# Final RMSNorm of a two-layer decoder trunk: square root on ScalarE and reciprocal on VectorE in place of logarithm and exponential on ScalarE

## The chip, the core and the metric

One core of a Trainium2 chip runs the whole program. The metric is the device time of one execution in microseconds (us), lower is better. The engines named below are TensorE (PE, and PEld for its weight loads), VectorE (DVE), ScalarE (ACT), GpSimd (POOL) and SyncE (SP, which here issues the stores of the output).

## The reference, cut to what matters

Two layers of token mixing, a SwiGLU FFN and a gated per-layer embedding are computed on a residual stream `x` of 1024 tokens by 1024 channels; a final RMSNorm then makes the output. Only the end of it matters here:

```python
def rmsnorm(x, g):
    xf = x.astype(jnp.float32)
    y = xf * lax.rsqrt(jnp.mean(xf * xf, axis=-1, keepdims=True) + EPS)
    return (y * g.astype(jnp.float32)).astype(x.dtype)

def hybrid_layer(...):
    ...
    hp = rmsnorm(x, norm_ple)
    x = x + jax.nn.sigmoid(hp @ w_ple_gate) * (p_i @ w_ple_proj)
    return x

def reference(...):
    for i in range(DEPTH):
        x = hybrid_layer(x, p[i], ...)
    return rmsnorm(x, norm_final)
```

## The kernel before

The residual stream lies in SBUF with channels on the partitions: `x` is 128 partitions by 8 channel chunks `c` by 1024 tokens. Tokens are worked on in two halves `h` of 512 (`hs(h)`). Each engine has its instructions in a fixed order, written out by hand, and they wait for one another by semaphores.

The last stage of a layer is `ple_gate`. TensorE makes 16 pieces of the gate, j = 0 to 15, in the order of `GATE_ORDER`: chunks 0 to 4 in both halves, then chunks 5, 6, 7 of half 0 (j = 10, 11, 12), then chunks 5, 6, 7 of half 1 (j = 13, 14, 15). A piece is 24 matmuls (eight chunks in three passes, L2194 to L2196). Each piece then goes back and forth between two engines:

- `gate_in(j)`, VectorE, L1233: the PSUM bank of the piece times the row scale, into `psg`;
- `gate_sigmoid(j)`, ScalarE, L1501: the sigmoid in place;
- `gate_out(j)`, VectorE, L1240 and L1242: the sigmoid times the embedding, added to `x`;
- `gate_square(j)`, ScalarE, L1508: the square of the new `x`, into one of two buffers;
- `gate_square(j)`, VectorE, L640 (`add_square`): the square added to `square_sum` of its half.

A matmul with a constant matrix sums `square_sum` over the partitions into a PSUM bank `aux`, which gives the mean of squares of every token of that half on all partitions: L2334 for half 0, and L2589 with the last two squares at L2592 for half 1.

In the last layer the final norm is woven into this stage. On ScalarE `root_half(DEPTH, 0, h)` makes `rstd[:, h, :]`, a tile of 128 by 512 in fp32, from the bank by two instructions: a logarithm with eps as its bias (L1488) and an exponential scaled by -0.5 (L1490). The signal `rstd_made` tells VectorE. On VectorE `result_part(h, chunks)` multiplies `x` by the gain and by `rstd` (L1256), one instruction for each chunk; after each SP stores 256 KB of the output (L2095). The orders are:

- ScalarE: squares 11 and 12, sigmoid 13, root of half 0, square 13, sigmoids 14 and 15, squares 14 and 15, root of half 1;
- VectorE: squares 11 and 12, `gate_in` 13, `gate_out` 13, results of half 0 for chunks 0 to 4, `gate_in` 14, `gate_out` 14, square 13, `gate_in` 15, result of chunk 5, `gate_out` 15, results of chunks 6 and 7, then all eight results of half 1.

ScalarE loads a table (ACT_TABLE_LOAD) ahead of a function that the loaded table doesn't hold; the program has no line for that, and the profile shows the load under the line of the function that needs it. VectorE has one other reciprocal in the program, L898, on a tile of 128 by 4 in the mLSTM part of each layer, between small instructions on the same tile (L893, L895, L906).

Of the kernel before, what the change touches and what calls it, by code (L numbers as in the profile page):

```python
# [10 lines left out]
ACT = mybir.ActivationFunctionType  # L11
# [7 lines left out]
DEPTH = 2  # L19
# [240 lines left out]
def build(nc, w_d, x_d, p_d, pos_d, const_d, par_d, early_d, out_d):  # L260
# [6 lines left out]
    with ExitStack() as ctx:  # L267
        def sb(name, shape, dt=F32):
            return ctx.enter_context(nc.sbuf_tensor(name, shape, dt))[:]

        def sem(name):
            return ctx.enter_context(nc.semaphore(name))
# [15 lines left out]
        rstd = sb("rstd", [P, 2, HALF])  # L288
# [69 lines left out]
        eps_c, one_c = small[:, 0:1], small[:, 1:2]  # L358
# [22 lines left out]
        aux_done = Signal(sem("aux_done"), AUX_FILLS)  # L381
# [37 lines left out]
        rstd_made = Signal(sem("token_rstd"), 6)  # L419
# [47 lines left out]
        def aux_at(L, name):  # L467

            return aux_done.at(L, AUX[name][1] + 1)

        def aux_read(name):

            return aux_emptied[AUX[name][0]].sem

        def aux_read_at(L, name):

            return aux_emptied[AUX[name][0]].at(L, AUX[name][2] + 1)
# [12 lines left out]
        def abank(name):  # L490
            return aux[:, AUX[name][0], :]

        def hs(half):
            return slice(HALF * half, HALF * half + HALF)
# [104 lines left out]
        def _(v):  # L599
# [651 lines left out]

            def result_part(h, chunks):

                v.wait_ge(rstd_made.sem, rstd_made.at(DEPTH, h + 1))
                for c in chunks:
                    v.scalar_tensor_tensor(x[:, c, hs(h)], x[:, c, hs(h)], mix_gain[:, c:c + 1], rstd[:, h, :],  # L1256
                                           ALU.mult, ALU.mult).then_inc(result, 1)

            def ple_gates(L):
# [25 lines left out]
                else:  # L1285
# [3 lines left out]
                    gate_in(L, 13)  # L1289
                    gate_out(L, 13)  # L1290
                    result_part(0, range(0, 5))
                    gate_in(L, 14)
                    gate_out(L, 14)
                    gate_square(L, 13)
                    gate_in(L, 15)
                    result_part(0, range(5, 6))
                    gate_out(L, 15)
                    result_part(0, range(6, 8))
                    result_part(1, range(KC))

# [61 lines left out]
            for L in range(DEPTH):  # L1362
                steps[0] = 0
                for item in MACRO:
# [55 lines left out]
                    elif what == "early_low":  # L1420
                        h = args[0]
# [5 lines left out]
                    elif what == "out_units":  # L1427
                        for part in reloaded:
                            v.wait_ge(part, L * 16 + 16)
                        for j in range(16):  # L1430
                            add_fill(L, U_OUT + j // 2, j % 2, j // 2, j % 2)
                            if j >= 1:
                                add_square(L, 0, j - 1)
                                c, h = divmod(j - 1, 2)
# [30 lines left out]
        def _(a):  # L1465
# [18 lines left out]
            def root_half(L, i, h):  # L1484

                name = ("row", i, h)
                a.wait_ge(aux_done.sem, aux_at(L, name))
                a.activation(rstd[:, h, :], abank(name), ACT.Ln, bias=eps_c).then_inc(aux_read(name), 1)  # L1488
                a.wait_ge(aux_read(name), aux_read_at(L, name))
                a.activation(rstd[:, h, :], rstd[:, h, :], ACT.Exp, scale=-0.5).then_inc(rstd_made.sem, 1)  # L1490

            def next_high(h, chunks):

                for c in chunks:
                    high_part(c, h, mix_gain[:, c:c + 1])

            def gate_sigmoid(L, j):

                m, h = GATE_ORDER[j]
                a.wait_ge(emptied[bank(U_GATE + m, h)].sem, emptied_at(L, U_GATE + m, h))  # L1500
                a.activation(psg[:, j % 2, :], psg[:, j % 2, :], ACT.Sigmoid).then_inc(ple_sig.sem, 1)  # L1501

            def gate_square(L, j):

                m, h = GATE_ORDER[j]
                a.wait_ge(x_ple.sem, x_ple.at(L, j + 1))
                a.wait_ge(sq_added.sem, sq_added.at(L, 32 + j - 1))
                a.activation(sqr[:, j % 2, :], x[:, m, hs(h)], ACT.Square).then_inc(sq_made.sem, 1)  # L1508

            def ple_gates(L):  # L1510

                for j in range(12):
                    m, h = GATE_ORDER[j]
                    if h == 0 and m <= 5:
                        units_high(L, U_GATE + m + 2)
                    gate_sigmoid(L, j)
                    if j >= 1:
                        gate_square(L, j - 1)
                gate_sigmoid(L, 12)
                if L < DEPTH - 1:  # L1520
                    next_high(0, range(0, 5))
                    gate_square(L, 11)
                    gate_sigmoid(L, 13)
                    units_high(L, UNITS)
                    next_high(0, range(5, 7))
                    gate_square(L, 12)
                    next_high(0, range(7, 8))
                    gate_sigmoid(L, 14)
                    units_high(L, UNITS + 1)
                    gate_square(L, 13)  # L1530
                    gate_sigmoid(L, 15)
                    gate_square(L, 14)
                    gate_square(L, 15)
                    next_high(1, range(KC))
                else:
                    gate_square(L, 11)
                    gate_square(L, 12)
                    gate_sigmoid(L, 13)
                    root_half(DEPTH, 0, 0)
                    gate_square(L, 13)  # L1540
                    gate_sigmoid(L, 14)
                    gate_sigmoid(L, 15)
                    gate_square(L, 14)
                    gate_square(L, 15)
                    root_half(DEPTH, 0, 1)

            def high_part(c, h, scale, to=None):

                a.activation(hh[:, c, hs(h)] if to is None else to, x[:, c, hs(h)], ACT.Copy,
                             scale=scale).then_inc(h_hi.sem, 1)  # L1550
# [14 lines left out]
            def units_high(L, last):  # L1565

                while told[0] <= UNITS * L + last and told[0] < UNITS * DEPTH:
                    l, u = divmod(told[0], UNITS)
                    raw_slot, value = LANDED[("unit", l, u)]
                    slot, held = TOOK[("unit", l, u)]  # L1570
                    n = columns(u)
                    for key in {k for k in held if k is not None}:
                        a.wait_ge(*consumed(key))
                    a.wait_ge(raw_landed[raw_slot], value)
                    to, whole = whi[:, slot, 0:n], raws[raw_slot][:, 0:n]
                    if u == U_GATES:
                        to = whi[:, slot, :].rearrange("p (k c) -> p k c", c=P)[:, :, 0:64]
                        whole = whole.rearrange("p (k c) -> p k c", c=64)
                    a.activation(to, whole, ACT.Copy).then_inc(unit_hi.sem, 1)  # L1579
                    told[0] += 1  # L1580
# [242 lines left out]
            for L in range(DEPTH):  # L1823
# [6 lines left out]
                for item in MACRO:  # L1830
# [15 lines left out]
                    elif what == "unit":  # L1846
# [9 lines left out]
                        if u == U_MQ + 1:  # L1856
# [5 lines left out]
                                         bias=one_c[0:MH]).then_inc(row_act.sem, 1)  # L1862
# [69 lines left out]
                    elif what == "pool":  # L1932
                        for j in range(2):
                            for h in range(2):
                                name = ("pm", j, h)
# [3 lines left out]
                    elif what == "turn":  # L1939
                        p = args[0]  # L1940
                        for h in range(2):
                            name = ("vt", p, h)
# [15 lines left out]
                    elif what == "ret_y":  # L1958
# [4 lines left out]
                        for h in range(2):  # L1963
                            name = ("ry", p, h)
# [6 lines left out]
                    elif what == "spread":  # L1971
                        p = args[0]
                        for h in range(2):
                            name = ("rv", p, h)
# [3 lines left out]
                        for h in range(2):  # L1978
                            name = ("rv", p, h)
                            a.wait_ge(aux_read(name), aux_read_at(L, name))  # L1980
                            a.activation(KZ[:, hs(h)], KZ[:, hs(h)], ACT.Exp, scale=-0.5).then_inc(ret_rstd.sem, 1)
                    elif what == "early_high":

                        h = args[0]
# [18 lines left out]
                    elif what == "out_units":  # L2003
                        a.wait_ge(h_ready.sem, h_ready.at(L, 32))
                        for j in range(16):
                            c, h = divmod(j, 2)
# [93 lines left out]
        def _(g):  # L2100
# [15 lines left out]
            def split(L, u):  # L2116
# [8 lines left out]
                if (L, u) == (0, 0):  # L2125

                    for q in range(2):
                        ks = slice(4 * q, 4 * q + 4)
                        hi, _, whole = gate_parts(ks, (0, raw_slot))
                        g.tensor_tensor(hi, whole, zero1[:, 0:1].unsqueeze(2).to_broadcast([P, 4, 64]),  # L2130
                                        ALU.add).then_inc(first_w, 1)
                        g.wait_ge(first_w, 2 * q + 1)
                        ins = gate_low(ks, (0, raw_slot))
                        ins.then_inc(first_w if q == 0 else weights_ready.sem, 1)
                    return
# [589 lines left out]
```

## Time and profile before

| What | us |
|---|---|
| time, median of 3 runs | 2439.54 (2439.28 to 2439.76) |
| time of the profiled execution | 2439.59 |
| span of the profiled execution, first to last instruction | 2437.8 |
| TensorE busy in it | 2414.3 (99%) |
| VectorE busy | 1529.6 (63%) |
| ScalarE busy | 972.3 (40%) |
| GpSimd busy | 1212.8 (50%) |

The span is counted from the first instruction to the last; 1.79 us of the execution's time lie around it. Busy time is the time in which an engine works on an instruction; waits and the issue of transfers don't count. The mean granted clock of TensorE over the span is 0.998 of full speed.

### The profile page before, as it was taken

The page shows a single profiled execution, that of the slowest core. Times are in us where ns is not written, and L with a number is a line of the kernel's source. Part 1 is how long each engine was busy: PE and PEld are TensorE (multiplying, and loading weights), DVE is VectorE, ACT ScalarE, POOL GpSimd, SP SyncE. Part 2 cuts the span into 40 slices and gives each one's busy share as a digit, 9 for nine tenths or more (in the row PEclk, how much of TensorE's full clock was granted, in tenths as well). Part 3 has the DMA queues.
Part 4 walks back from the last instruction along what each step waited for, and adds up shares of the span by engine and source line. Part 5 has one row for each costly group of instructions (what it writes and reads, how often), then busy time and mean ns, then how long its engine had stood idle before and what let it go on. Part 6 is the DMA issues. An engine that isn't in the chain of part 4 may idle for free.

```text
span 2437.8 us, 30233 instructions
## 1 busy us (share of the span) xinstructions
PE 2414.3 (99%) x11528; PEld 1992.8 (82%) x11528; DVE 1529.6 (63%) x1955; ACT 972.3 (40%) x1428; POOL 1212.8 (50%) x768
## 2 busy tenths in 40 slices
PE   8999999999999999999999999999999999999998
PEld 6888878888888878888878887888888888888886
DVE  8967846555444467675596778546545444776745
ACT  5323334433333343446333352335333333343553
POOL 2211212278788868882122112222888788698710
PEclk9999999999999999999999999999999999999999
DMA  4342222123233255332143322312223233545211
GB/s 174 102 100 59 74 76 96 35 91 108 95 121 108 87 186 165 126 125 70 39 158 98 81 57 70 98 59 69 88 90 108 92 119 112 190 146 165 78 52 69
DMA packets 108415, 245.92 MB, mean 101 GB/s; under 512 B 35688, under 2 KB 44136, under 8 KB 104432
## 3 DMA queue, kind: packets, MB, share of 16 engines
q1 hardware_dynamic: 60880, 126.90, 17.0%
q10 hardware_dynamic: 47392, 117.09, 14.5%
q8 instruction: 92, 1.51, 0.3%
q14 instruction: 51, 0.42, 0.1%
HBM read 179.43 MB, written 51.41 MB: 95 GB/s over the span
## 4 chain that ended last, share of the span: by engine, by line
PE 60%; DVE 2%; ACT 1%; issue 0%; POOL 0%; ACTq 0%; DVEq 0%; POOLq 0%
PE proj L2194 9%; PE proj L2196 9%; PE proj L2195 9%; PE proj L2292 3%; PE proj L2291 3%; PE proj L2290 3%; PE proj L2258 3%; PE aux L2258 3%; PE proj L2256 3%; PE aux L2256 3%; PE aux L2257 3%; PE proj L2257 3%; PE aux L2292 2%; PE aux L2291 2%; PE aux L2290 2%; DVE h_lo L622 0%
## 5 line engine op out<-in xcount | busy, mean ns | idle before, releaser
L2146 POOL TENSOR_TENSOR w_lo<-w_raw,w_hi 128x1024 fp32r<-128x1024 f32 x98 | 255.6, 2609 | 932.0 <-ACT w_hi L1579 919.4
L2194 PE MATMUL proj<-h_hi,w_hi 128*128 128x512 f32 x1376 | 547.0, 398 | 1.4 <-POOL w_lo L2146 0.9
L2196 PE MATMUL proj<-h_lo,w_hi 128*128 128x512 f32 x1376 | 536.5, 390 | 0.0
L2195 PE MATMUL proj<-h_hi,w_lo 128*128 128x512 f32 x1376 | 536.4, 390 | 0.0
L2153 POOL TENSOR_TENSOR w_lo<-w_raw,w_hi 128x512 fp32r<-128x512 f32 x180 | 273.9, 1525 | 119.5 <-ACT w_hi L1561 119.5
L2153 POOL TENSOR_TENSOR w_lo<-turns,w_hi 128x512 fp32r<-128x512 f32 x180 | 268.6, 1494 | 89.2 <-ACT w_hi L1561 89.2
L2194 PEld LDWEIGHTS proj<-h_hi,w_hi 128*128 128x128 f32 x1376 | 258.7, 188 | 58.6 <-issue 4.8
L2195 PEld LDWEIGHTS proj<-h_hi,w_lo 128*128 128x128 f32 x1376 | 258.8, 188 | 54.3 <-issue 2.9
L2196 PEld LDWEIGHTS proj<-h_lo,w_hi 128*128 128x128 f32 x1376 | 258.6, 188 | 54.3
L1561 ACT ACTIVATE w_hi<-turns 128x512 fp32r<-128x512 f32 x180 | 113.1, 628 | 227.9 <-PE proj L2258 99.1
L1561 ACT ACTIVATE w_hi<-w_raw 128x512 fp32r<-128x512 f32 x180 | 112.3, 627 | 223.7 <-PE aux L2258 93.2
L1579 ACT ACTIVATE w_hi<-w_raw 128x1024 fp32r<-128x1024 f32 (+1 forms) x99 | 103.6, 1048 | 215.4 <-PE proj L2196 98.2
L1310 DVE TENSOR_TENSOR x<-x,proj 128x1024 f32<-128x1024 f32 x80 | 97.4, 1218 | 54.8 <-PE proj L2292 54.2
L2256 PE MATMUL proj<-h_hi,w_hi 128*128 128x512 f32 x320 | 124.6, 389 | 0.0
L2258 PE MATMUL aux<-h_lo,w_hi 128*128 128x512 f32 x320 | 124.6, 389 | 0.0
L2257 PE MATMUL proj<-h_hi,w_lo 128*128 128x512 f32 x320 | 124.6, 389 | 0.0
L2258 PE MATMUL proj<-h_lo,w_hi 128*128 128x512 f32 x320 | 124.6, 389 | 0.0
L2256 PE MATMUL aux<-h_hi,w_hi 128*128 128x512 f32 x320 | 124.6, 389 | 0.0
L2257 PE MATMUL aux<-h_hi,w_lo 128*128 128x512 f32 x320 | 124.6, 389 | 0.0
L1310 DVE TENSOR_TENSOR x<-x,aux 128x1024 f32<-128x1024 f32 x60 | 72.9, 1216 | 41.8 <-PE aux L2292 41.8
L1137 DVE TENSOR_TENSOR act<-act,silu_g 128x512 f32<-128x512 f32 x88 | 78.9, 934 | 31.7 <-ACT silu_g L1597 31.6
L1078 DVE TENSOR_TENSOR x<-x,proj 128x512 f32<-128x512 f32 x64 | 42.6, 679 | 82.5 <-PE proj L2196 82.2
(330 smaller groups left out, 5330.0 us busy)
## 6 DMA issues: line engine op xcount, KB each, us to landing
w_raw<-weights SPq DMA_DIRECT2D x160, 512.0 KB, 3.5
turns<-weights SPq DMA_DIRECT2D x60, 512.0 KB, 3.8
act_sums_spill<-rows ACTq DMA_DIRECT2D x20, 1024.0 KB, 6.9
h_whole<-act_sums_spill ACTq DMA_DIRECT2D x40, 512.0 KB, 3.8
act_sums_spill<-act ACTq DMA_DIRECT2D x20, 512.0 KB, 5.2
ffn_b_whole<-act_sums_spill ACTq DMA_DIRECT2D x20, 512.0 KB, 5.0
act_sums_spill<-act ACTq DMA_DIRECT2D x20, 256.0 KB, 4.3
ffn_bw_whole<-act_sums_spill ACTq DMA_DIRECT2D x10, 512.0 KB, 4.1
```

The costliest lines, as they stand in the source:

```text
L1310: v.tensor_tensor(to, to, bank_of, ALU.subtract if i in (3, 5) else ALU.add).then_inc(down_added.sem, 1)
L1561: a.activation(operand_slot(L, b, i)[0], block_weights(L, b)[i], ACT.Copy).then_inc(operand_hi.sem, 1)
L2146: g.tensor_tensor(wlo[:, slot, 0:n], w, whi[:, slot, 0:n].bitcast(F32), ALU.subtract).then_inc(weights_ready.sem, 1)
L2153: g.tensor_tensor(lo, block_weights(L, b)[i], hi.bitcast(F32), ALU.subtract).then_inc(operand_ready.sem, 1)
L2194: pe.matmul(out, wh, rhi, start=first, stop=False)
L2195: pe.matmul(out, wl, rhi, start=False, stop=False)
L2196: return pe.matmul(out, wh, rlo, start=False, stop=final)
L2256: pe.matmul(out, wh[:, o], hi, start=first and j == 0, stop=False, skip_group_check=True)
L2257: pe.matmul(out, wl[:, o], hi, start=False, stop=False, skip_group_check=True)
L2258: ins = pe.matmul(out, wh[:, o], lo, start=False, stop=j == 3, skip_group_check=True)
L2290: pe.matmul(out[:, e, :], wh[:, o], hi, start=first and n == 0, stop=False, skip_group_check=True)
L2291: pe.matmul(out[:, e, :], wl[:, o], hi, start=False, stop=False, skip_group_check=True)
```

## The change

For the final norm alone, `root_half` is replaced on ScalarE by `last_deviation`, which makes the square root of mean plus eps in one instruction. VectorE takes the reciprocal of that tile in place, at the head of the first `result_part` of each half, and gives the signal `rstd_made` itself. `root_half` stays in use at the start of the program, and the norms in between use `root`, which isn't changed.

```diff
             def result_part(h, chunks):
 
+                if 0 in chunks:
+                    name = ("row", 0, h)
+                    v.wait_ge(aux_read(name), aux_read_at(DEPTH, name))
+                    v.reciprocal(rstd[:, h, :], rstd[:, h, :]).then_inc(rstd_made.sem, 1)
                 v.wait_ge(rstd_made.sem, rstd_made.at(DEPTH, h + 1))
                 for c in chunks:
...
+            def last_deviation(h):
+
+                name = ("row", 0, h)
+                a.wait_ge(aux_done.sem, aux_at(DEPTH, name))
+                a.activation(rstd[:, h, :], abank(name), ACT.Sqrt, bias=eps_c).then_inc(aux_read(name), 1)
+
...
                     gate_sigmoid(L, 13)
-                    root_half(DEPTH, 0, 0)
+                    last_deviation(0)
                     gate_square(L, 13)
...
                     gate_square(L, 15)
-                    root_half(DEPTH, 0, 1)
+                    last_deviation(1)
```

## Rows read from the trace of the kernel before

**Rows 1.** The page's part 1: engine, busy us (share), instructions.

```profile
span 2437.8 us, 30233 instructions
PE 2414.3 (99%) x11528; PEld 1992.8 (82%) x11528; DVE 1529.6 (63%) x1955; ACT 972.3 (40%) x1428; POOL 1212.8 (50%) x768
```

**Rows 2.** The chain that ended last, from 2410.3 us: start, length, what.

```profile
2410.47 0.70 DVE ple_sig L1233
...
2413.13 0.69 ACT rstd L1488
...
2415.80 3.40 DVE x L1256 x5
...
2422.52 0.70 DVE ple_sig L1233
...
2425.36 0.63 ACT squares L1508
...
2428.01 1.28 ACT L1490
...
2431.38 3.98 DVE x L1256 x6
```

**Rows 3.** Waits between engines, 2405 to 2440 us: total, times, longest.

```profile
DVE x L1256 <- ACT rstd L1490: 5.8, 2, 3.3
```

**Rows 4.** ScalarE in order of time, last 28 us: start, length [idle before <-releaser].

```profile
2411.84 1.28 ACT L1488 ACT_TABLE_LOAD   x1
2413.13 0.69 ACT L1488 ACTIVATE rstd<-aux,small 128x512 f32<-128x512 f32 x1
2413.84 1.28 ACT L1490 ACT_TABLE_LOAD   x1
2415.13 0.63 ACT L1490 ACTIVATE rstd<-rstd 128x512 f32<-128x512 f32 x1
2415.67 0.61 ACT L1508 ACTIVATE squares<-x 128x512 f32<-128x512 f32 x1
2416.31 1.28 ACT L1501 ACT_TABLE_LOAD   x1
2419.83 0.64 ACT L1501 ACTIVATE ple_sig<-ple_sig 128x512 f32<-128x512 f32 x1 [2.25 <-DVE ple_sig L1233]
...
2427.30 0.69 ACT L1488 ACTIVATE rstd<-aux,small 128x512 f32<-128x512 f32 x1
```

**Rows 5.** VectorE in order of time, the same stretch.

```profile
2412.58 0.69 DVE L1242 TENSOR_TENSOR x<-x,ple_t 128x512 f32<-128x512 f32 x1
2415.80 3.40 DVE L1256 SCALAR_TENSOR_TENSOR x<-x,early,rstd 128x512 f32<-128x512 f32 x5 [2.53 <-ACT rstd L1490]
2419.12 0.68 DVE L1233 TENSOR_TENSOR ple_sig<-proj,rstd 128x512 f32<-128x512 f32 x1
...
2421.23 0.69 DVE L1242 TENSOR_TENSOR x<-x,ple_t 128x512 f32<-128x512 f32 x1
2421.84 0.68 DVE L640 TENSOR_TENSOR square_sum<-square_sum,squares 128x512 f32<-128x512 f32 x1
...
2429.96 5.39 DVE L1256 SCALAR_TENSOR_TENSOR x<-x,early,rstd 128x512 f32<-128x512 f32 x8 [3.31 <-ACT rstd L1490]
```

**Rows 6.** TensorE in order of time: the last matmuls of pieces 14 and 15.

```profile
2416.65 0.39 PE L2196 MATMUL proj<-h_lo,w_hi 128*128 128x512 f32 x1
...
2422.09 0.39 PE L2196 MATMUL proj<-h_lo,w_hi 128*128 128x512 f32 x1
```

**Rows 7.** Small VectorE instructions on the tile `small`: duration ns shortest/median/longest.

```profile
L893 DVE SCALAR_TENSOR_TENSOR small<-ml_num x16: 153/155/1532, 144.0 to 1450.8; 128x4 f32<-128x4 f32 x16
L895 DVE TENSOR_TENSOR small<-small,ml_cols x16: 161/163/165, 144.1 to 1452.3; 128x4 f32<-128x4 f32 x16
L898 DVE RECIPROCAL small<-small x16: 177/178/179, 144.3 to 1452.5; 128x4 f32<-128x4 f32 x16
...
L906 DVE TENSOR_SCALAR small<-small x16: 169/1660/2135, 145.7 to 1453.9; 128x4 f32<-128x4 f32 x16
```

**Rows 8.** Groups of VectorE instructions by line and shape: busy us, mean ns.

```profile
L1242 DVE TENSOR_TENSOR x<-x,ple_t 128x512 f32<-128x512 f32 x32 | 22.1, 692 | 1.1
...
L708 DVE TENSOR_SCALAR ang<-ang 128x512 f32<-128x512 f32 x2 | 0.9, 427 | 0.1
...
L935 DVE COPY rows<-mix 128x1 f32<-128x1 f32 x4 | 0.6, 142 | 0.0
```

**Rows 9.** GpSimd in order of time, 2380 us to the end: its last instruction.

```profile
2392.51 2.39 POOL L2146 TENSOR_TENSOR w_lo<-w_raw,w_hi 128x1024 fp32r<-128x1024 f32 x1 [8.49 <-ACT w_hi L1579]
```

## The prediction

> **What bounds the kernel now.** I read the page's first part, then the chain that ended last, then the engines' order of time over the last 28 us. TensorE is busy for 99% of the span [rows 1], so what VectorE and ScalarE do is hidden almost everywhere. The change touches only the end, and there the cover runs out. Piece 15 of the gate, TensorE's last product of weights, ends at 2422.09 + 0.39 = 2422.48 us [rows 6], and 15.3 us of the span follow it. In that stretch the chain hops between VectorE and ScalarE [rows 2], and one wait stands out: VectorE's results wait for `rstd` twice, 5.8 us together, the longest 3.3 us [rows 3]. The reader is to see two places. In half 0 the chain runs through the root (2413.13) and the five results (2415.80) to `gate_in` 15 at 2422.52; in half 1 from the last square (2425.36) through the second load (2428.01) to the last results [rows 2].
>
> **Taken away.** In each half, ScalarE's second table load, 1.28 us, and the exponential, 0.63 us [rows 4]. In half 0 VectorE's results start at 2415.80, which is 1.98 us after the logarithm's end at 2413.13 + 0.69 = 2413.82 [rows 4, 5]. In half 1 the logarithm ends at 2427.99 and the results start at 2429.96, 1.97 us later [rows 4, 5].
>
> **Kept.** The first load (1.28 us) and an activation that reads the PSUM bank with eps as bias. The square root isn't in the trace; I take the logarithm's 0.69 us, the same engine, shape, source and bias. The sigmoid's 0.64 us without a bias [rows 4] is the other end, and the difference of 0.05 us is nothing here. In half 0 the square root's table must be followed by a square and then by the sigmoid's table. If the square isn't held beside the square root, one more load of 1.28 us comes ahead of square 13; ScalarE idles 2.25 us before sigmoid 14 and also loses 1.91 us of work [rows 4], so it is hidden: zero. Without that cover it would cost 1.28 us. In half 1 no square follows.
>
> The row shows two loads in each root, one at the logarithm and one at the exponential [rows 4]. The Trainium skill ("ScalarE: Activation LUTs", Table sets: the hidden batching unit) says that logarithm and exponential share a set and need one load. By that rule the change would have no load to remove, and its sum would be 2 x 1.28 = 2.56 us worse than the one below; the trace disagrees, and the two loads are what I count.
>
> **Added.** One reciprocal of 128x512 on VectorE in each half, R us, at the head of the results. VectorE picks up ScalarE's last result 0.04 us after it: 2415.13 + 0.63 = 2415.76 to 2415.80 [rows 4, 5]; I take the same 0.04 us again from the reciprocal to the first result. So the results start at 2413.86 + R + 0.04 = 2413.90 + R in half 0, against 2415.80, and at 2428.07 + R in half 1, against 2429.96. The change breaks even in either half at R = 1.9 us.
>
> What is queued behind VectorE's new wait is the five results, then `gate_in` 14. TensorE has had piece 14 ready since 2416.65 + 0.39 = 2417.04, while `gate_in` 14 starts at 2419.12 [rows 5, 6]: it comes behind the results, so it moves with them. From there to the last square each step waits for the one before it on the other engine, so a delay goes through one for one. A gain doesn't: `gate_in` 15 starts at 2422.52 [rows 2], 0.04 us after TensorE ended piece 15. VectorE alone, at the pace of 0.61 us from 2421.23 to 2421.84 [rows 5], could have started it at 2422.45, so half 0 has 0.07 us of slack and nothing to win. SP's stores come behind the results and move with them; the last results and stores keep their length. GpSimd, whose last instruction ends at 2394.90 [rows 9], is idle. So the change is
>
> max(0, R - 1.90 - 0.07) + (R - 1.89) us.
>
> **The size of R.** The trace has a reciprocal of 128x4 alone: 178 ns [rows 7]. The price per element is that less a fixed part, divided by 4, and the fixed part must come from other instructions. An element of an ordinary instruction takes (692 - 163)/508 = 1.04 ns [rows 7, 8]. The bounds, by the row that lends the fixed part:
> - The reciprocal runs at an ordinary pace and its fixed part is just longer: 178 - 4 = 174 ns, R = 0.174 + 512 x 1.04 ns = 0.71 us. At the pace of the 128x512 TENSOR_SCALAR, 427 ns [rows 8], R = 0.43 us; that is the lowest end.
> - The TENSOR_SCALAR of 128x4, undisturbed 169 ns [rows 7]: fixed 165, (178 - 165)/4 = 3.3 ns, R = 1.85 us.
> - The TENSOR_TENSOR, 163 ns [rows 7]: fixed 159, 4.8 ns, R = 2.6 us.
> - The SCALAR_TENSOR_TENSOR, 155 ns [rows 7]: fixed 151, 6.8 ns, R = 3.63 us.
> - The COPY of 128x1, 142 ns [rows 8]: fixed 141, 9.25 ns, R = 4.88 us, the upper end.
>
> I take 3.63 us. The reciprocal is the slowest of the four small ones though it reads one operand, which speaks for a price per element; and L893 is the shortest of the three that work on the same tile two steps away, so the least of a fixed part that this place has shown. It is the choice that carries the forecast.
>
> **Sum.** Half 0: 3.63 - 1.97 = +1.66 us. Half 1: 3.63 - 1.89 = +1.74 us. Together +3.40 us. The profiled execution took 2439.59 us, its span plus 1.79 us, and stands 0.05 us from the median of 2439.54; on the median the forecast is 2442.94, say 2442.9 us, +0.14%. A measurement of this kernel can tell about 0.2%, 4.9 us, from no change, so this counts as no change though slower by the middle of it.
>
> **Rivals.**
> *The reciprocal runs at one element a step.* R = 0.71 us: half 0 gains nothing (TensorE's piece 15 takes over as the wait), half 1 gains 1.18 us: 2438.4 us; with R = 0.43 us, 2438.1. For it: 178 ns is only 9 ns above the TENSOR_SCALAR. Against: no row has a fixed part of 174 ns. With R up to 1.9 the time stays at or below 2439.6. Chance 0.2. The Trainium skill bears on it ("Vector Engine (DVE) Microarchitecture Reference", 4.2 Triggers, successor indices, and repeat count): a repeat count is measured in elements taken in, not in cycles, so a repeat alone needn't slow the stream; the trace, at 128x4, leaves this open.
>
> *Eight steps an element.* VectorE becomes the bound of both halves: 8 x 1.04 = 8.33 ns, fixed 178 - 33 = 145 ns, R = 4.41 us, and the change is 2.44 + 2.52 = +4.96 us: 2444.5 us; with the upper end of R it is +5.9, 2445.4. This is the side that is measurably slower, and it decides from R = 4.37 us, where the sum passes 4.88 us. For it: a fixed part of 145 ns lies near the COPY's 141. Against: the three instructions on the same tile have 151 to 165. Chance 0.18. The Trainium skill speaks for it ("VectorE: DVE Perf Modes", First, the fixed hardware budget): the reciprocal is an iterated division with a repeat count of 8. That rule read as eight cycles an element gives this rival's time; the trace can't confirm it at 128x4.
>
> *The change doesn't do what it says:* ScalarE loads two tables ahead of the square root, or waits where it didn't. With one more load in half 1, 2442.9 + 1.3 = 2444.2 us. Nothing in the rows asks for it: the load at L1488 comes right behind sigmoid 13 [rows 4] and the square root stands in the same place. Chance 0.02.
>
> **How the numbers follow.** The forecast's case, R between 1.9 and 4.37 us (2439.6 to 2444.4), has 0.6, the three others 0.2, 0.18 and 0.02. The predicted time is that of R = 3.63 us. The range takes in both ends of R, 2438.1 to 2445.4 us: either rival has near 0.2, so neither can be left out alone with the bounds still held. Faster by over 0.2% would need 4.9 us, and with R = 0 the change gives 1.9: 0.01. Slower by over 0.2% is the second rival: 0.18. Within 0.2%: 0.81.
>
> **What would show it.** In the changed kernel's profile: one load and one activation on `rstd` in each half; RECIPROCAL 128x512 with its length, which alone decides; the results of half 0 starting at 2413.90 + R and of half 1 at about 2429.73 + R, for 2428.07 + R plus the 1.66 us handed down; `gate_in` 15 waiting for TensorE if R is under 1.97 us and behind VectorE's own queue if above. The forecast is wrong if R is under 1.9 or over 4.37 us, or if half 0's delay doesn't reach half 1, which would halve the sum.

## The result and the profile after

| | before | after |
|---|---|---|
| median, us | 2439.55 (20 runs) | 2442.57 (20 runs) |
| ratio to before | 1 | 1.0013, 95% interval 1.0007 to 1.0019 |
| profiled execution, us | 2439.59 | 2444.08 |
| its span, us | 2437.8 | 2442.3 |
| VectorE busy, us | 1529.6 | 1536.6 |
| ScalarE busy, us | 972.3 | 968.4 |

The change makes the kernel 3.02 us slower by the medians, 0.13%. That is clear of no change by the interval, and less than the 0.2% that the prediction set as the bound of a difference. The forecast was 2442.9 us. Three of the kernels below, and the kernel before in one of its series, have one execution each that took hundreds or thousands of us longer, and the medians leave it out. ScalarE does 3.9 us less work, which is two table loads and two exponentials; VectorE does 7.0 us more, of which the two reciprocals are 6.7.

The profiled execution after lies 1.5 us above its median, and part of its distance from the one before has nothing to do with the change. The granted clock of TensorE was 0.83 between 30 and 40 us, against 1.00 in the profile before; at 140 us the execution was 1.44 us behind (VectorE's L742 at 141.50 against 140.06), and 1.01 us of that were left at the start of `gate_in` 13, ahead of the first instruction that the change touches. So times of the end are compared below from that common mark: 2410.47 us before [rows 2], 2411.48 after, an offset of 1.01 us.

ScalarE in order of time, the kernel after (start, length, instruction, in brackets the idle time before it and who ended it):

```profile
2412.85 1.28 ACT L1500 ACT_TABLE_LOAD   x1
2414.15 0.69 ACT L1500 ACTIVATE rstd<-aux,small 128x512 f32<-128x512 f32 x1
2414.73 0.62 ACT L1518 ACTIVATE squares<-x 128x512 f32<-128x512 f32 x1
2415.37 1.28 ACT L1511 ACT_TABLE_LOAD   x1
...
2427.73 0.63 ACT L1518 ACTIVATE squares<-x 128x512 f32<-128x512 f32 x1 [0.96 <-DVE x L1242]
2428.38 1.28 ACT L1500 ACT_TABLE_LOAD   x1
2430.35 0.69 ACT L1500 ACTIVATE rstd<-aux,small 128x512 f32<-128x512 f32 x1 [0.69 <-PE aux L2602]
```

Against [rows 4] the second load and the exponential are gone in both halves, the square root takes the logarithm's 0.69 us, and square 13 follows it with no load between. New is the last line: the square root of half 1 stands 0.69 us waiting for TensorE's row. VectorE in order of time, the kernel after:

```profile
2411.48 0.69 DVE L1233 TENSOR_TENSOR ple_sig<-proj,rstd 128x512 f32<-128x512 f32 x1
...
2414.87 3.35 DVE L1257 RECIPROCAL rstd<-rstd 128x512 f32<-128x512 f32 x1 [0.59 <-ACT rstd L1500]
2418.26 3.40 DVE L1260 SCALAR_TENSOR_TENSOR x<-x,early,rstd 128x512 f32<-128x512 f32 x5
...
2424.90 0.68 DVE L1233 TENSOR_TENSOR ple_sig<-proj,rstd 128x512 f32<-128x512 f32 x1
...
2431.07 3.35 DVE L1257 RECIPROCAL rstd<-rstd 128x512 f32<-128x512 f32 x1 [2.05 <-ACT rstd L1500]
2434.45 5.39 DVE L1260 SCALAR_TENSOR_TENSOR x<-x,early,rstd 128x512 f32<-128x512 f32 x8
```

The reciprocal takes 3.35 us, against the 1.90 us of load, exponential and handover that it replaces. Less the offset, half 0's results start at 2417.25 where [rows 5] have 2415.80 (+1.45); `gate_in` 15 at 2423.89 where [rows 2] have 2422.52 (+1.37); the last square at 2426.72, against 2425.36 (+1.36); half 1's results at 2433.44, against 2429.96 (+3.48). So the 4.49 us between the two profiled executions are 1.01 of the start, 1.36 of half 0, 0.68 of the new wait on TensorE and, as what is left, 1.44 of half 1. That wait was in no part of the forecast. TensorE in order of time, the kernel after:

```profile
2423.08 0.39 PE L2206 MATMUL proj<-h_lo,w_hi 128*128 128x512 f32 x1
2425.03 1.13 PE L2599 MATMUL aux<-square_sum,const 128*128 128x512 f32 x2 [1.57 <-DVE square_sum L640]
2426.82 3.49 PE L2602 MATMUL aux<-squares,const 128*128 128x512 f32 x4 [0.66 <-ACT squares L1518]
```

Piece 15 isn't delayed, since TensorE doesn't need VectorE for it; the sum of squares that the row matmul L2599 needs is. So TensorE idles 1.57 us; L2599 still takes 1.13 us behind that, and then the last four row matmuls stretch to 3.49 us. Busy time of each engine and the granted clock in stretches of two us, the kernel after (columns: length; busy of PE, PEld, DVE, ACT, POOL; clock; DMA share; GB/s):

```profile
2424.00:2426.00 2.00, 0.97 (x2) 0.30 (x2) 2.00 (x4) 0.39 (x1) 0.00 (x0) 1.00 0.00 0
2426.00:2428.00 2.00, 1.34 (x3) 0.50 (x2) 1.93 (x4) 1.04 (x3) 0.00 (x0) 0.62 0.34 131
2428.00:2430.00 2.00, 2.00 (x4) 0.61 (x2) 1.02 (x2) 1.64 (x2) 0.00 (x0) 0.53 0.38 150
```

The clock falls from its upper level (2.4 GHz, 1.00) to its lower one (1.2 GHz, 0.50) after the idle stretch, behind L2599 and ahead of the matmuls that half 1's square root waits for.

### The profile page after: what moved, and what is told of

Read it like the earlier page. It is cut to its first block, busy times and chain, and to the rows that moved or that the text cites. A ratio compares the mean times of both kernels' runs of the same rounds, so it can differ in the third digit from the quotient of the medians.

```text
span 2442.3 us, 30231 instructions
## 1 busy us (share of the span) xinstructions
PE 2415.8 (99%) x11528; PEld 1993.0 (82%) x11528; DVE 1536.6 (63%) x1957; ACT 968.4 (40%) x1424; POOL 1214.9 (50%) x768
## 4 chain that ended last, share of the span: by engine, by line
PE 60%; DVE 2%; ACT 1%; issue 0%; POOL 0%; DVEq 0%; ACTq 0%; POOLq 0%
PE proj L2204 9%; PE proj L2206 9%; PE proj L2205 9%; PE proj L2300 3%; PE proj L2302 3%; PE proj L2301 3%; PE aux L2267 3%; PE proj L2268 3%; PE aux L2268 3%; PE proj L2267 3%; PE proj L2266 3%; PE aux L2266 3%; PE aux L2300 2%; PE aux L2302 2%; PE aux L2301 2%; DVE h_lo L622 0%
```

## The experiments

The theory: each half pays on the chain by itself, the difference between the reciprocal and what it replaced, as in the prediction's formula. The rivals: half 0's part is hidden, or gains where R is short; the new wait costs by itself; and the clock on TensorE has a part in the sum. Three steps try them: one half at a time, another length of the added instruction, and TensorE kept busy. A fourth uses what they show.

### One half at a time

```diff
-                if 0 in chunks:
+                if 0 in chunks and h == 0:
...
-                    last_deviation(1)
+                    root_half(DEPTH, 0, 1)
```

> Square root and reciprocal in half 0 only; half 1 keeps logarithm and exponential. Theory (each half pays on the chain by itself): the reciprocal of 3.35 us takes the place of the 1.90 us that the second load and the exponential took, less 0.07 us of slack before piece 15: +1.38 us on 2439.55, so 2440.9 us. Clock theory on top: VectorE's delay opens a gap of some 1.5 us on TensorE between piece 15 and the row matmul at L2599, the granted clock falls to its lower level there, and half 1's logarithm waits up to 0.7 us for the row; then up to 2441.6 us, and the wait is in the profile. Rival (half 0's delay is hidden behind TensorE's last piece): no difference, 2439.6 us.

2440.92 us against 2439.54, +1.38 (ratio 1.0006, interval 0.9997 to 1.0015). ScalarE in its profile:

```profile
2425.98 0.63 ACT L1518 ACTIVATE squares<-x 128x512 f32<-128x512 f32 x1 [0.96 <-DVE x L1242]
2426.63 1.28 ACT L1492 ACT_TABLE_LOAD   x1
2428.57 0.69 ACT L1492 ACTIVATE rstd<-aux,small 128x512 f32<-128x512 f32 x1 [0.66 <-PE aux L2602]
```

The wait on TensorE is here too, though half 1 is as before: it comes with half 0's delay, not from the square root. VectorE in the same profile:

```profile
2409.73 0.69 DVE L1233 TENSOR_TENSOR ple_sig<-proj,rstd 128x512 f32<-128x512 f32 x1
...
2423.15 0.69 DVE L1233 TENSOR_TENSOR ple_sig<-proj,rstd 128x512 f32<-128x512 f32 x1
...
2431.23 5.39 DVE L1260 SCALAR_TENSOR_TENSOR x<-x,early,rstd 128x512 f32<-128x512 f32 x8 [3.96 <-ACT rstd L1494]
```

This execution reached the mark at `gate_in` 13 0.74 us ahead of the kernel before. From the mark `gate_in` 15 starts at 2423.89, +1.37, as the theory has it, and half 1's results at 2431.97, +2.01, since the wait on TensorE comes on top. So that the median stands at just +1.38 is partly luck: the profiled executions of all these kernels reach the mark between 2409.73 and 2411.89 us.

The other half alone has the same edit turned round (`h == 1`, and `root_half(DEPTH, 0, 0)` kept).

> Square root and reciprocal in half 1 only; half 0 keeps logarithm and exponential. Theory: +1.46 us (3.35 less 1.89), 2441.0 us; TensorE's last piece and its row matmuls lie as in the kernel before, so no clock falls ahead of the row and the square root doesn't wait for TensorE. Rival (half 0 pays nothing and half 1 all): +3.0 us, 2442.6 us. Rival (the stores at the end hide a later start): under +1 us.

2440.88 us, +1.34 (ratio 1.0006, interval 0.9997 to 1.0016). VectorE in its profile:

```profile
2410.46 0.69 DVE L1233 TENSOR_TENSOR ple_sig<-proj,rstd 128x512 f32<-128x512 f32 x1
...
2422.49 0.69 DVE L1233 TENSOR_TENSOR ple_sig<-proj,rstd 128x512 f32<-128x512 f32 x1
...
2427.99 3.35 DVE L1257 RECIPROCAL rstd<-rstd 128x512 f32<-128x512 f32 x1 [1.37 <-ACT rstd L1500]
2431.38 5.39 DVE L1260 SCALAR_TENSOR_TENSOR x<-x,early,rstd 128x512 f32<-128x512 f32 x8
```

`gate_in` 15 stands where it stood before, the square root waits for nobody, and from the mark half 1's results start at 2431.39, 1.43 us later than before. The two halves add up: 1.37 + 1.43 = 2.80 by these places, without the wait on TensorE, and 1.38 + 1.34 = 2.72 by the medians, against 3.02 for both. Each interval alone takes in no change, so it is the places in the profiles that carry this; the medians agree with them to some 0.1 us.

### Another length

```diff
-                    v.reciprocal(rstd[:, h, :], rstd[:, h, :]).then_inc(rstd_made.sem, 1)
+                    v.tensor_tensor(rstd[:, h, :], rstd[:, h, :], rstd[:, h, :], ALU.mult).then_inc(rstd_made.sem, 1)
```

> The changed kernel with rstd times itself (a product of two tensors) in place of the reciprocal, so the values of the output are others; all waits stay. Theory (the length of the reciprocal alone decides): R is 0.69 us, half 0 gains nothing since gate_in 15 then waits for TensorE, half 1 gains 1.20 us: 2438.3 us. Rival (both halves gain): -2.4 us, 2437.2 us. Rival (the wait and the handover to VectorE cost by themselves): 2439.5 us or more.

2438.29 us against 2439.54, -1.25 (ratio 0.9996, interval 0.9987 to 1.0005). VectorE in its profile:

```profile
2411.89 0.69 DVE L1233 TENSOR_TENSOR ple_sig<-proj,rstd 128x512 f32<-128x512 f32 x1
...
2415.28 0.69 DVE L1257 TENSOR_TENSOR rstd<-rstd 128x512 f32<-128x512 f32 x1 [0.59 <-ACT rstd L1500]
...
2423.91 0.69 DVE L1233 TENSOR_TENSOR ple_sig<-proj,rstd 128x512 f32<-128x512 f32 x1 [1.18 <-PE proj L2206]
...
2430.15 5.39 DVE L1260 SCALAR_TENSOR_TENSOR x<-x,early,rstd 128x512 f32<-128x512 f32 x8
```

Half 0's results come early, and `gate_in` 15 then waits 1.18 us for TensorE's piece 15: that is the floor under half 0. From the mark (an offset of 1.42 us) it starts at 2422.49, where it stood before, and half 1's results start at 2428.73, 1.23 us sooner: all of the gain is half 1's. The theory had 1.20, so the handover to VectorE costs nothing by itself.

The next edit takes the reciprocal of half the columns.

```diff
-                    v.reciprocal(rstd[:, h, :], rstd[:, h, :]).then_inc(rstd_made.sem, 1)
+                    v.reciprocal(rstd[:, h, 0:256], rstd[:, h, 0:256]).then_inc(rstd_made.sem, 1)
```

> The changed kernel with the reciprocal of only 256 of the 512 columns of rstd in each half, so the other columns stay square roots. Theory: R is 1.75 us, just under the break-even of 1.9: half 0 nothing, half 1 -0.14 us, so 2439.4 us, no difference from the kernel before. Rival (the price is a fixed one of an instruction on a tile of this kind): as the changed kernel, 2442.4 us.

2439.23 us against 2439.49 (ratio 0.9998, interval 0.9989 to 1.0007): no difference. VectorE in its profile:

```profile
2409.93 0.69 DVE L1233 TENSOR_TENSOR ple_sig<-proj,rstd 128x512 f32<-128x512 f32 x1
...
2427.47 1.75 DVE L1257 RECIPROCAL rstd<-rstd 128x256 f32<-128x256 f32 x1 [1.37 <-ACT rstd L1500]
2429.26 5.39 DVE L1260 SCALAR_TENSOR_TENSOR x<-x,early,rstd 128x512 f32<-128x512 f32 x8
```

From the mark half 1's results start at 2429.80, 0.16 us sooner than before, where the theory had 0.14. So the same edit, with the same waits, is almost without effect just under the break-even that the prediction put at 1.9 us, and the price goes by the columns.

The price itself was taken from a row of sizes behind the last result:

```diff
                     result_part(1, range(KC))
+                    at_c = 0
+                    for n in (4, 16, 64, 128, 256):
+                        v.reciprocal(pt[:, 0, at_c:at_c + n], rstd[:, 0, 0:n])
+                        at_c += n
...
```

> The changed kernel with small instructions behind the last result on VectorE, into a tile that nobody reads: reciprocals of 128 by 4, 16, 64, 128 and 256, and a multiplication by a constant (TENSOR_SCALAR) of 128 by 4 and 256. Theory (a price per element and a fixed part): from 178 ns at 4 and 3352 ns at 512 the line is 153 ns + 6.25 ns an element, so 253, 553, 953 and 1753 ns at 16, 64, 128 and 256. Rival (the long one has a cost that the short ones lack, a start or a port, and 6.25 is not the price per element): off the line by over 5%. The time of the kernel means nothing, since the extra instructions end after the last store.

Groups of VectorE instructions, last 17 us (busy us, mean ns):

```profile
L1257 DVE RECIPROCAL rstd<-rstd 128x512 f32<-128x512 f32 x1 | 3.4, 3352 | 2.2 <-ACT rstd L1506 2.2
L1306 DVE RECIPROCAL ple_t<-rstd 128x256 f32<-128x256 f32 x1 | 1.7, 1696 | 0.0
L1306 DVE RECIPROCAL ple_t<-rstd 128x128 f32<-128x128 f32 x1 | 0.9, 896 | 0.0
L1306 DVE RECIPROCAL ple_t<-rstd 128x64 f32<-128x64 f32 x1 | 0.5, 496 | 0.0
...
L1306 DVE RECIPROCAL ple_t<-rstd 128x16 f32<-128x16 f32 x1 | 0.2, 222 | 0.0
L1306 DVE RECIPROCAL ple_t<-rstd 128x4 f32<-128x4 f32 x1 | 0.2, 172 | 0.0
```

From 64 to 128 to 256 each element costs (896 - 496)/64 = 6.25 and (1696 - 896)/128 = 6.25 ns, the slope that 178 ns at 4 and 3352 ns at 512 give too. The fixed part was expected at 153 ns, and the reciprocal of 256 columns that stands behind a wait, in the run above, lies on that line: 1752 and 1754 ns. These, back to back with nothing to wait for, lie under it: by 12% at 16, 10% at 64, 6% at 128 and 3% at 4 and 256. The rival's sign, off the line by over 5%, is there at three of the five, but not for its reason, since from 64 on the slope holds and the fixed part is 96 ns (496 - 64 x 6.25). So the slope is right, and the fixed part is another behind a wait than without one; why, no run shows. In element times of 1.04 ns [rows 7, 8] it is 6.0, neither one nor eight.

### TensorE kept busy

```diff
+            for _ in range(2):
+                pe.matmul(aux[:, 2, :], mean_all, acc[:, 0, :], start=True, stop=True)
             pe.wait_ge(sq_added.sem, sq_added.at(DEPTH, -2))
```

> The changed kernel with two more 128x512 matmuls into an unused PSUM bank behind piece 15, where TensorE otherwise idles 1.57 us. Clock theory: the granted clock stays at its upper level through the row matmuls, the square root of half 1 doesn't wait for TensorE, and the time is what the chain alone gives, 2442.4 us or a little under, with less spread than 2441.8 to 2444.9. Rival (the clock falls there whatever TensorE does, or the wait is the row's own length): the wait of some 0.7 us stays and the time is 2442.6 us or more, since the extra matmuls stand ahead of the row.

2442.39 us against 2439.54, +2.85 (ratio 1.0012, interval 1.0003 to 1.0021). TensorE, and then the stretch of the row matmuls, in its profile:

```profile
2422.32 1.88 PE L2598 MATMUL aux<-square_sum,const 128*128 128x512 f32 x4
2424.05 1.12 PE L2601 MATMUL aux<-square_sum,const 128*128 128x512 f32 x2
2425.84 1.13 PE L2604 MATMUL aux<-squares,const 128*128 128x512 f32 x2 [0.66 <-ACT squares L1518]
2427.43 1.12 PE L2604 MATMUL aux<-squares,const 128*128 128x512 f32 x2 [0.47 <-ACT squares L1518]
```

```profile
2426.00:2428.00 2.00, 1.53 (x4) 0.43 (x4) 1.98 (x3) 1.24 (x2) 0.00 (x0) 1.00 0.34 131
```

With the gap filled the clock stays at its upper level through the row, each of its pairs of matmuls takes 1.12 or 1.13 us, and the square root of half 1 starts right behind its table load:

```profile
2427.39 1.28 ACT L1500 ACT_TABLE_LOAD   x1
2428.69 0.69 ACT L1500 ACTIVATE rstd<-aux,small 128x512 f32<-128x512 f32 x1
```

The profiled execution of 2442.42 us is 2.83 above the one before: the sum of the two halves, with nothing over. The executions weren't clearly closer together, 2441.78 to 2444.04 us against 2441.76 to 2444.87 of the changed kernel. To see whether this also lowers the median, the changed kernel and this one were run once more side by side.

> The changed kernel once more, beside the next one on the same chip. Clock theory: where the gap of 1.57 us on TensorE behind piece 15 falls together with the clock's fall ahead of the last two row matmuls, the square root of half 1 waits some 0.65 us, and the executions scatter from 2441.8 to 2443.1 us apart from those that start late; median 2442.5 us.

> The changed kernel with two more matmuls behind piece 15, on the same chip. Clock theory: no wait on the row, the median 0.1 to 0.6 us under the changed kernel's and the executions closer together, about 2442.3 us. Rival (the fall costs the median nothing): the same median as the changed kernel to 0.1 us.

2442.53 and 2442.43 us against 2439.58. The difference of 0.10 us lies where theory and rival meet, so it decides nothing between them, and the expected closer spread isn't there: 2441.89 to 2444.09 us and 2441.71 to 2443.62. The changed kernel's profile in that run:

```profile
2425.27 1.12 PE L2599 MATMUL aux<-square_sum,const 128*128 128x512 f32 x2 [1.58 <-DVE square_sum L640]
2427.05 1.13 PE L2602 MATMUL aux<-squares,const 128*128 128x512 f32 x2 [0.66 <-ACT squares L1518]
2428.64 1.12 PE L2602 MATMUL aux<-squares,const 128*128 128x512 f32 x2 [0.47 <-ACT squares L1518]
```

```profile
2426.00:2428.00 2.00, 1.34 (x3) 0.30 (x2) 1.93 (x4) 1.04 (x3) 0.00 (x0) 1.00 0.33 129
```

The same gap of 1.58 us, and this time the clock stayed at its upper level and nobody waited. So the gap doesn't bring the fall every time: of four profiles with it (after, half 0 alone, the row of sizes, and this one) three show the fall and a wait of 0.7 to 0.9 us, while none of the three without it that pay for the reciprocal (half 1 alone, TensorE kept busy, twice) shows either. In the medians filling the gap is worth 0.2 and 0.1 us, which these runs can't tell from nothing. Were the fall in three of every four executions, with 0.7 us lost each time, the median would stand higher than that, so the share of three in four isn't to be carried over to all executions. What decides it in one stays open.

### One activation in place of two

The experiments say that half 0 has nothing to win and that half 1 wins what shortens the way from row to result. ScalarE can do it in one function, with nothing new on VectorE; the edit is to the kernel before:

```diff
+            def one_root(h):
+
+                name = ("row", 0, h)
+                a.wait_ge(aux_done.sem, aux_at(DEPTH, name))
+                a.activation(rstd[:, h, :], abank(name), ACT.Abs_reciprocal_sqrt, bias=eps_c).then_inc(rstd_made.sem, 1)
...
-                    root_half(DEPTH, 0, 0)
+                    one_root(0)
...
-                    root_half(DEPTH, 0, 1)
+                    one_root(1)
```

> The kernel before with one activation, the reciprocal square root of mean plus eps (Abs_reciprocal_sqrt), in place of logarithm and exponential in both halves of the final norm; VectorE does nothing new. Theory: half 1 loses the second load and the exponential, -1.93 us, half 0 gains nothing since gate_in 15 waits for TensorE: 2437.6 us. Rival (a second load or a longer activation comes with this function): at or over 2438.9 us. Rival (both halves gain): 2435.7 us.

> One activation (reciprocal square root) in both halves, on another chip or at another time. Theory: 2437.6 us, 1.9 us under the kernel before, half 0 nothing and half 1 all. Rival: at or over 2439 us.

2438.08 us against 2439.49 (ratio 0.9994, interval 0.9985 to 1.0003), and 2437.60 against 2439.58 (0.9992, 0.9983 to 1.0001), where 2437.6 was expected both times. ScalarE, and then VectorE, in the first of the two profiles:

```profile
2427.28 1.28 ACT L1496 ACT_TABLE_LOAD   x1
2428.57 0.69 ACT L1496 ACTIVATE rstd<-aux,small 128x512 f32<-128x512 f32 x1
```

```profile
2411.74 0.69 DVE L1233 TENSOR_TENSOR ple_sig<-proj,rstd 128x512 f32<-128x512 f32 x1
...
2423.79 0.69 DVE L1233 TENSOR_TENSOR ple_sig<-proj,rstd 128x512 f32<-128x512 f32 x1 [1.94 <-PE proj L2202]
...
2429.29 5.39 DVE L1256 SCALAR_TENSOR_TENSOR x<-x,early,rstd 128x512 f32<-128x512 f32 x8 [1.37 <-ACT rstd L1496]
```

From the mark at `gate_in` 13 (offset 1.27 us), half 1's results start at 2428.02, 1.94 us sooner than before, and `gate_in` 15 waits 1.94 us for TensorE: half 0's gain is lost whole. By its medians this version is below both kernels, by 1.4 and 2.0 us under the one before; its intervals still reach 1, so against the kernel before that rests on the places in the profile.

## Why the prediction was right, and what it missed

- *Where the kernel is bound, and that half 0 hands its delay on:* right. With the measured R of 3.352 us the prediction's formula gives 1.38 + 1.46 = 2.84 us, 2442.39 us. By the places in the profiles half 0 alone gave 1.37 up to `gate_in` 15 and half 1 alone 1.43; the kernel with TensorE kept busy took 2442.39 and 2442.43.
- *That a gain in half 0 is worth nothing:* right, shown by the waits of 1.18 and 1.94 us on piece 15, and the break-even near 1.9 us agrees with the 1.75 us reciprocal, which gained 0.16 us.
- *The square root's cost:* right: 0.69 us, one load, and no load ahead of square 13.
- *The size of R, the term that carried the forecast:* 3.63 was taken, 3.35 measured, 8% too much, 0.56 us in the sum. The row that lent the fixed part came nearest: the measured line has 178 - 4 x 6.25 = 153 ns, where L893 lends 151 [rows 7]. That was partly luck, for no run shows that a reciprocal shares another instruction's fixed part, and without a wait it was 96. And 2 ns of the 178, spread over four elements, is 0.5 ns an element, and over 512 elements 0.26 us. Four elements were the whole lever arm; the other rows' ends, 0.43 and 4.88 us, show how loose it was.
- *Both rivals on the size of R* fell: 6.25 ns an element is neither the 8.33 of eight steps, which would have been measurably slower, nor the 1.04 of one element a step. The Trainium skill ("VectorE: DVE Perf Modes", First, the fixed hardware budget) gives a repeat count of 8; read as eight cycles it doesn't give the time measured here.
- *Missed:* the prediction followed the delay along VectorE and ScalarE and named the results, `gate_in` 14 and the stores as what stands behind it. It didn't name TensorE's row matmul L2599, which also waits for VectorE, for the square that is added behind `gate_out` 14. Its wait of 1.57 us is a gap on TensorE, and in the profiles of three kernels with it the clock fell in that place and cost 0.7 to 0.9 us. The first profile's sum needs that term; the medians need 0.1 to 0.2 us of it, if any.

The forecast median of 2442.94 and the measured 2442.57 are close in part by luck, because two errors of opposite sign met: 0.56 us too much for R, some 0.2 us too little for the row.

## What to carry to other kernels

Before swapping one instruction for another of a different engine, find a price per element, not the duration of a tiny one: from a 128x4 row the 128x512 reciprocal could have been anything from 0.4 to 4.9 us, and the sign of the change hung on 1.9. Where a stage hops between engines beside a long stream on TensorE, a delay can go through while a gain stops at the stream's next piece, as in half 0 here, so work out each direction by itself. And when a chain is delayed, ask which idle stretches that opens on the other engines too.

## What the runs showed of the hardware

- VectorE's reciprocal of fp32 costs 6.25 ns an element, six times an ordinary two-operand instruction's 1.04 ns, behind a wait at 4, 256 and 512 elements (178, 1752 to 1754 and 3352 ns) and back to back from 64 to 256; the fixed part was 153 ns behind a wait and 96 ns back to back.
- ScalarE loads one table for the square root and one for Abs_reciprocal_sqrt, 1.28 us each, and squares ran behind either without another load; logarithm and exponential took two [rows 4].
- TensorE idled 1.5 to 1.6 us behind its long stream and ran one pair of row matmuls in 1.13 us. Behind that pair it was granted its lower clock in three of four profiles, where the two pairs that followed, 1.12 us each at the upper level, took 3.46 to 3.68 us together. In the fourth, with the same gap, it kept its upper level.
